# Heads' sums of squares in two column quarters of TensorE, and a spread matrix of 128 rows

## The reference

```python
def rms_norm(x, g):
    xf = x.astype(jnp.float32)
    y = xf * lax.rsqrt(jnp.mean(xf * xf, axis=-1, keepdims=True) + RMS_EPS)
    return (y * g.astype(jnp.float32)).astype(x.dtype)
...
    q_b = rms_norm(q_b.reshape(b, l, B_HEADS, B_HEAD_DIM), qn_g)
    k_b = rms_norm(k_b.reshape(b, l, B_KV_HEADS, B_HEAD_DIM), kn_g)
...
    q = l2_normalize(to_heads(q)) * (HEAD_DIM ** -0.5)
    k = l2_normalize(to_heads(k))
...
    o = o * lax.rsqrt(jnp.mean(o * o, axis=-1, keepdims=True) + NORM_EPS) * norm_w.astype(jnp.float32)
```

## Time and profile before

| | us |
|---|---|
| median of three runs | 2885.03 |
| the three runs | 2883.73, 2885.03, 2910.47 |
| profiled execution, its own time | 2913.37 |
| its span in the trace | 2911.6 |
| PE busy | 2786.7 |
| DVE busy | 1809.9 |
| ACT busy | 1246.7 |

### The profile page before, as it was taken

How to read it: one execution, slowest core, us unless ns; L and a number is a source line. 1 busy time by engine, 2 the same in 40 slices (tenths; PEclk the granted TensorE clock), 3 DMA queues, 4 the chain that set the end, 5 groups by cost and what they waited for, 6 DMA issues and landing times.

```text
span 2911.6 us, 50366 instructions
## 1 busy us (share of the span) xinstructions
PE 2786.7 (96%) x22070; PEld 2638.8 (91%) x22070; DVE 1809.9 (62%) x2229; ACT 1246.7 (43%) x1375; POOL 270.2 (9%) x330
## 2 busy tenths in 40 slices
PE   6899999998999999989999999989999999999998
PEld 3598877797988998989999999979999999999998
DVE  2358767688777545566556555795666665466653
ACT  4323444345443334444434448453544443344444
POOL 0022002120111000003113110021000000000000
PEclk9899999998999999999999999999999999999999
DMA  9867535574776554435555544430445555555553
GB/s 368 325 226 247 194 133 201 202 277 149 251 247 225 192 199 162 169 136 190 174 173 175 174 167 146 154 139 1 145 160 188 189 181 188 189 184 187 183 185 138
DMA packets 93034, 546.84 MB, mean 188 GB/s; under 512 B 12656, under 2 KB 12816, under 8 KB 47888
## 3 DMA queue, kind: packets, MB, share of 16 engines
q1 hardware_dynamic: 69552, 466.39, 45.3%
q0 software_dynamic: 20480, 67.13, 6.8%
q10 hardware_dynamic: 2784, 10.11, 0.9%
HBM read 541.48 MB, written 2.10 MB: 187 GB/s over the span
## 4 chain that ended last, share of the span: by engine, by line
PE 67%; DVE 6%; ACT 2%; issue 2%; DMA 1%; DVEq 0%; ACTq 0%
PE bank L727 67%; DVE r L2156 2%; DVE f L2727 1%; ACT r L1459 1%; PE bank L787 1%; DVE f L2193 0%; DMA f<-in_later 0%; DVE f L2791 0%; ACT f L1821 0%; DVE f L2788 0%; DVE f L2804 0%; DVE f L2780 0%; DVE f L2539 0%; DMA f<-in_units 0%; DVE f L2556 0%
## 5 line engine op out<-in xcount | busy, mean ns | idle before, releaser
L727 PE MATMUL bank<-r,r 128*128 128x256 f32 (+1 forms) x19596 | 2444.1, 287 | 44.8 <-DVE r L2156 20.5
L727 PEld LDWEIGHTS bank<-r,r 128*128 128x128 f32 x19596 | 2376.2, 190 | 100.8 <-DVE r L2156 28.2
L2156 DVE TENSOR_TENSOR r<-f,r 128x2048 fp32r<-128x2048 f32 (+2 forms) x447 | 961.1, 2151 | 724.4 <-ACT r L1459 723.1
L1459 ACT CAST r<-f 128x2048 fp32r<-128x2048 f32 (+2 forms) x447 | 792.7, 1775 | 886.4 <-PE bank L727 684.2
L727 PE MATMUL bank<-f,f 128*128 128x128 f32 (+10 forms) x1992 | 326.5, 375 | 58.2 <-DMA f<-in_units 23.1
L727 PEld LDWEIGHTS bank<-f,f 128*128 128x128 f32 (+3 forms) x1992 | 218.8, 177 | 121.7 <-issue 53.1
L2193 DVE SCALAR_TENSOR_TENSOR f<-f,f,f 128x512 f32<-128x512 f32 x240 | 179.8, 749 | 53.8 <-DMA f<-in_later 38.2
L3052 POOL DMA_DIRECT2D f<-in_later x256 | 137.5, 537 | 799.8 <-DVE f L2193 475.8
L2727 DVE SCALAR_TENSOR_TENSOR f<-f,f,f 128x255 f32<-128x255 f32 (+1 forms) x272 | 132.9, 491 | 8.8
L1476 ACT COPY f<-bank 128x512 f32<-128x512 f32 x149 | 83.9, 584 | 115.6 <-PE bank L727 109.3
L3061 POOL TENSOR_TENSOR f<-f,f 32x512 f32<-32x512 f32 x24 | 62.7, 2614 | 658.4 <-DVE f L2665 658.4
(11 more groups left out here) (235 smaller groups left out, 925.2 us busy)
## 6 DMA issues: line engine op xcount, KB each, us to landing
f<-in_units SPq DMA_DIRECT2D x346, 1024.0 KB, 4.8
f<-in_units SPq DMA_DIRECT2D x124, 768.0 KB, 4.3
f<-in_later POOLq DMA_DIRECT2D x256, 256.0 KB, 4.3
f<-in_units SPq DMA_DIRECT2D x8, 576.0 KB, 4.4
f<-in_x ACTq DMA_DIRECT2D x2, 1024.0 KB, 12.8
f<-in_ctx ACTq DMA_DIRECT2D x2, 1024.0 KB, 12.2
f<-in_x_turned ACTq DMA_DIRECT2D x1, 2048.0 KB, 13.4
out<-f SPq DMA_DIRECT2D x4, 256.0 KB, 3.7
```

The costliest lines, as they stand in the source:

```text
L727: return e.matmul(o, lhsT, rhs, start=start, stop=stop, skip_group_check=True)
L1459: e.copy(unit_view(high[HIGH_OF[u]][1], u), unit_view(raw[RAW_OF[u]][0], u)).then_inc(*up("w_hi", ("hi", u)))
L2156: e.tensor_tensor(unit_view(raw[RAW_OF[u]][1], u), unit_view(raw[RAW_OF[u]][0], u), unit_view(high[HIGH_OF[u]][1], u).bitcast(F32), ALU.su ...
```

## The change

The sums of even tiles go to row 0 and up, those of odd tiles to row 32 and up, in output rows and columns of the array 0 to 31 and 32 to 63. The left operand has 32 columns of which column i // 2 is one. So the root, the reciprocal and both parts of the factors have 64 rows, and the spread matrix has 128 rows, with ones in the rows of a head's two parts. The fill of `hrr` goes, since all its rows are written. The constant `pick` grows by 64 columns, so what lies behind it in K moves by 256 bytes; KEEP grows by 32 floats, so R moves by 128 bytes and keeps its remainder modulo 128 bytes.

```diff
-KEEP = 9360
+KEEP = 9392
...
-    pick = np.zeros((128, 64), np.float32)
+    pick = np.zeros((128, 128), np.float32)
+    for x in range(4):
+        pick[:, 32 * x + x] = 1.0
+    spread = np.zeros((128, 1024), np.float32)
     for h in range(8):
-        pick[:, 8 * h + h] = 1.0
-    spread = np.zeros((40, 1024), np.float32)
-    for h in range(8):
-        spread[h, 128 * h:128 * h + 128] = 1.0
-        spread[32 + h, 128 * h:128 * h + 128] = 1.0
+        for row in (32 * (h % 2) + h // 2, 64 + 32 * (h % 2) + h // 2):
+            spread[row, 128 * h:128 * h + 128] = 1.0
...
-        cs, hr = cs[0:32, :, :], cs[32:40, 0, :]
+        cs, hr = cs[0:32, :, :], cs[64:128, 0, :]
...
                 e.wait_ge(*at("hrs sq", name, i))
-                mm(e, o[0:8, 0:T], C["pick"][:, 8 * i:8 * i + 8], tmps[i % len(tmps)][:, 0:T], i == 0, i == tiles - 1).then_inc(
+                row, x = 32 * (i % 2), 32 * (i // 2)
+                mm(e, o[row:row + 32, 0:T], C["pick"][:, x:x + 32], tmps[i % len(tmps)][:, 0:T], i < 2, i >= tiles - 2).then_inc(
                     *up("pe_norm", ("hrs mm", name, i), ("ps", "hrs", name)))
...
-                ins = mm(e, o[:, x * T:(x + 1) * T], spread[0:40, h * 128:(h + 1) * 128], hrr[0:40, slot, :], x == 0, True)
+                ins = mm(e, o[:, x * T:(x + 1) * T], spread[:, h * 128:(h + 1) * 128], hrr[:, slot, :], x == 0, True)
...
-            e.activation(hr, ps("hrs", name)[0:8, 0:T], ACT.Sqrt, bias=eps[0:8, :], scale=scale).then_inc(
+            e.activation(hr, ps("hrs", name)[0:64, 0:T], ACT.Sqrt, bias=eps[0:64, :], scale=scale).then_inc(
...
-            e.tensor_copy(hrr[32:40, slot, :], hr).then_inc(*up("dve_norm"))
+            e.tensor_copy(hrr[64:128, slot, :], hr).then_inc(*up("dve_norm"))
...
-            e.tensor_tensor(hrr[0:8, slot, :], hr, hrr[32:40, slot, :].bitcast(F32), ALU.subtract).then_inc(
+            e.tensor_tensor(hrr[0:64, slot, :], hr, hrr[64:128, slot, :].bitcast(F32), ALU.subtract).then_inc(
...
-            e.tensor_copy(hrr[0:40, :, :], C["spread"][64:104, 0:3 * T].rearrange("p (a b) -> p a b", a=3)).then_inc(*up("dve_norm"))
-            e.tensor_copy(spread[0:40, :], C["spread"][0:40, :]).then_inc(*up("dve_norm"))
+            e.tensor_copy(spread[:, :], C["spread"]).then_inc(*up("dve_norm"))
```

## The result

The changed kernel takes 2926.41 us (median of 4 runs, 2924.99 to 2928.41) against 2887.92 us before (4 runs, one more than ahead of the prediction): a recorded ratio of 1.0118, 95% interval 1.0064 to 1.0171. It is slower, and outside the range. The span of the profiled execution is 2924.6 us; before it was 2911.6, but that execution had gone through its last stage at the longer of the two steps of the earlier trace rows.

What follows compares the result with a forecast made beforehand. TensorE, busy 96% of the 2911.6 us span, was taken as the bound; sums 4.5 plus spread 0.7 gave 5.2 us off the 2885.0 median, so 2879.8 us, range 2872 to 2909.

Steps and rivals of the forecast that it cites:

- The sums: Pick sums run side by side save 4.5 us: qb 0.86, dlk 0.96, dlq 0.97, osum 1.73, kb 0.
- a pair costs 0.43 us, where it cost 0.86: Two fp32 pick matmuls in two column quarters overlap; bounds 0 and 0.43 us gained per pair.
- the path that was named: dlq: PE's 4.39 us wait is for DVE, whose transposes wait until PE uses its last unit; 0.97 us gain kept.
- The rival of pairs that don't overlap: Pick sums: pairs don't overlap since each waits and increments; only the spread's 0.7 us go, 2884.3; chance 0.1.
- The spread: Spread matmuls with 128 rows avoid changeovers around their groups: 8 sides x 0.09 = 0.7 us, bounds 0 and 1.8.
- The whole: Whole kernel: sums 4.5 plus spread 0.7 give 5.2 us saved; bounds 0 and about 10.
- The clock: Half-clock stretches of 3 to 7 us after PE waits may come or go: 2 to 3.5 us either way.
- The step that failed: Layout: queues and the rest put at nothing, so the sum had no term for moving working tensors by 128 bytes.
- Addresses: working tensors move by 128 bytes: Rival: ordinary matmuls' step follows addresses; 12,400 short-stepped ones could go long, 56 us, 2936; chance 0.05.
- The two paces of the last stage: Last stage, some 6,200 matmuls, goes at a short or long step, 28 us apart; two of three runs had short.
- The rival that put the median at 2908: Last stage draws the long step in most runs of the new kernel: 2879.8 + 28 = 2908; chance 0.2.

Runs made afterwards that it cites:

- full change in old places: All the change's matmuls and rows, but a 64-column pick matrix read through overlapping windows, KEEP 9360, so K and R stay; 2879.44 us against 2887.68 for the kernel before.

## Why the prediction was wrong

**The sums, right.** The step "a pair costs 0.43 us, where it cost 0.86" measured 0.40 less per free pair, 0.94 in dlk and in dlq (0.96 and 0.97 said), 1.69 in osum (1.73 said), 0.08 in qb's middle and in kb (0 said for both). 2 x 0.40 + 0.08 for qb, 0.08 for kb, 0.94 twice and 1.69 are 4.5 us, as forecast, with small misses that cancel. dlq's gain came by the path that was named. In the full change in old places its sums start at 1939.40 as before, and the root hardly sooner (1943.01 against 1943.05, since ACT loads a table until then), but DVE's transposes start at 1949.03 in place of 1950.17. The rival of pairs that don't overlap fell. The Trainium skill's rule of some 26 ns for each increment of tiles side by side ("TensorE: Matmul & The Clock Gate", section "The cost: per-tile semaphore tail") does not show in PE's own time: osum's eight waves take 1.85 us, which is 8 x 0.216 and one changeover of 0.1, as in the earlier trace rows, where quarters share one increment. It may show where an engine waits for the sums. ACT's root began 0.416 us after the start of osum's last sum in the kernel before, and 0.452 after it in the changed one; for qb it was 0.417 and 0.453. That is 0.036 us, once in a norm, near one increment of that rule, but the root also reads 64 partitions in place of 8, and no run separates the two.

**The spread, right in kind.** The changeovers are gone (window above). Their price was read at half: 0.09 us is the first of two long steps, and both together cost 0.20. By that the term is some 8 x 0.20 = 1.6 us and not 0.7 (an estimate: where PE has just waited, only the second step is saved), still below what a total can show.

**The whole, in old places, right in size.** Predicted 5.2 us; measured 8.2 between medians, 5 to 8 within the groups of times, and 5 to 32 us by the interval of the ratio, which the two paces of the last stage widen.

**The clock, inside its bounds.** In the full change in old places PE's wait for dlq's factors is 2.93 us in place of 4.39, and the stretch behind it runs at a granted clock of 1.00 where it had 0.50. But the stretch ahead of it, from 1949.8 to 1955.1, has 0.68 where it had 1.00. Behind the wait 26 matmuls take 3.07 us where 25 took 5.70; ahead of it 32 take 5.47 us where they took 3.84. So such stretches moved both ways, by 2.6 and 1.6 us.

**The step that failed** is the one that put moving R at nothing: the sum has no term for it, and "Addresses: working tensors move by 128 bytes" had a chance of 0.05. I took the remainder modulo 128, which the change keeps, for the one that matters; the runs show that the remainder modulo 256 of R's distance to the weights does: with R alone moved, the kernel before went from 2887.68 to 2931.75 us. The size was about right: 12,400 short steps of a median run going long were priced at 56 us, 2936, and the kernel came to 2926. The chance was not. My evidence against was that one tensor goes at both paces. That is so, but it shows only that the good distance allows both. It says nothing of a distance that allows one. The evidence for it was in the same rows: a 4% wide difference in step, unexplained, over 18,648 matmuls, next to a change that moved one operand of nearly all of them. With a term of 28 us left unexplained, 0.05 was too low.

**The two paces of the last stage, right.** Two paces, 28 us apart, are the two groups of times (the profile at distance 192 with the short step has a span of 2878.3). All seven profiles of kernels with all weights at distance 192 bear it out: the three that took over 2900 us have the long step there, the four below 2892 the short one. The rival that put the median at 2908 by them had its condition met and its price wrong. The changed kernel's profile has the long step there, and its four runs lie within 3.4 us. But that was not one draw of two: at distance 64 the long step came in the other stages too, so the time was 2926.

**What stays open.** Why a distance of 192 allows the short step and others don't, and what picks the step at a break. It is not chance everywhere: from 1420 to 1680 us the kernel before and the changed kernel with R moved by 256 bytes switch between short and long at the same places of the program, in one pattern that repeats (174 short, 5 long, 30 short, 1 long, 105 short, 196 long, and so on). Each triple of matmuls reads high weights with high activations, high with low, and low with high. With high weights alone at distance 64, and with low ones alone, the short step still came, so the distance of a matmul's own two operands does not decide by itself; only all weights at 64 shut the short step out. Why moving the high ones costs some 14 to 17 us while moving the low ones gains isn't shown. The runs moved the weights' half of this, never high and low activations apart: that was not tried.

## What to carry to other kernels

When a change touches the layout of SBUF, compare the step between starts of the bulk matmuls before and after, in one long window: here 4.5 ns in each of 5,000 outweighed an edit worth 5 us. If runs of one kernel fall in two groups, look for a stage with two paces before anything is compared by medians. And a constant that would grow can sometimes be read through overlapping windows, as the narrow pick matrix here, so that nothing behind it moves.

## What the runs showed of the hardware

- The step of a stream of 128x128 by 256 fp32r matmuls at full granted clock depends on the distance, modulo 256 bytes, between the activations and all the weight buffers in SBUF: means of 0.1133, 0.1167, 0.1178, 0.1183, 0.1187 or 0.1200 us in one stage here. A move of both together by 128 bytes gave the old median back (2893.50 against 2888.81).
- The long step is as long while DVE and ACT are idle and no DMA packet is in flight (0.1177 against 0.1178 us).
- At distance 192 the last stage goes at 0.1133 or 0.1178, and keeps the short one over more than 5,600 matmuls. With the low weights 128 bytes off, none of 21 runs has a time of the long one, nor have ten runs with the buffers' order alone changed.
- fp32 matmuls in two column quarters run side by side even if each waits and increments: 0.22 us a wave for both.
- A changeover between 40-row and 128-row left operands costs about 0.20 us in two steps, 0.21 and 0.23 where the ordinary ones take 0.113 to 0.118.
